# An HGRN block and a retention block on one core: one more pair of projection units in Winograd form in the first mixer, and the order of three ScalarE instructions in the MLPs

## What is computed

```python
def first_block(x, ...):
    h = rmsnorm(x, norm_mix)
    q, f, i, g = split(h @ w_in, 4)                  # w_in is 1024 x 4096
    log_f = logaddexp(log(lb), log1p(-lb) + log_sigmoid(f))
    k = (1 - lb) * sigmoid(-f)
    o = hgrn2_chunk_scan(silu(q) * 128 ** -0.5, k, i, log_f)   # 8 heads of 128
    x = x + (headnorm(o) * out_norm * silu(g)) @ w_out
    a = relu(rmsnorm(x, norm_mlp) @ w1)
    x = x + (a * a) @ w2
    return rmsnorm(x, norm_final)

def second_block(x, ...):                            # convolution and retention
    h = x + hybrid_mixer(rmsnorm(x, norm1), ...)
    h = h + sq_relu_mlp(rmsnorm(h, norm2), w_up, w_down)
    return rmsnorm(h, final_norm)
```

## Time and profile before

| | |
|---|---|
| median of 3 runs | 2258.19 us (2257.88 to 2261.65) |
| profiled execution: time, span | 2260.37 us, 2258.6 us |
| mean granted TensorE clock | 0.998 |
| busy: TensorE | 2244.6 us, 99%, 10744 instructions |
| busy: VectorE | 1682.2 us, 74% |
| busy: GpSimd | 1256.8 us, 56% |
| busy: ScalarE | 951.9 us, 42% |
| chain that ended last | TensorE 95%, VectorE 3%, VectorE's queue 1% |

### The profile page before, as it was taken

How to read it: one execution, slowest core, us unless ns; L and a number is a source line. 1 busy time by engine, 2 the same in 40 slices (tenths; PEclk the granted TensorE clock), 3 DMA queues, 4 the chain that set the end, 5 groups by cost and what they waited for, 6 DMA issues and landing times.

```text
span 2258.6 us, 32472 instructions
## 1 busy us (share of the span) xinstructions
PE 2244.6 (99%) x10744; PEld 1879.4 (83%) x10744; DVE 1682.2 (74%) x2355; ACT 951.9 (42%) x1565; POOL 1256.8 (56%) x1420
## 2 busy tenths in 40 slices
PE   9999999999999999999999999999999999999998
PEld 7888888888888888888888888888888888888887
DVE  7887887856878777876666877765787787787766
ACT  6355544424634533543432224322453454344433
POOL 4544552344556566655546666763556665666562
PEclk9999999999999999999999999999999999999999
DMA  4011111023264556455313111112335645554553
GB/s 158 29 38 38 33 34 47 29 93 130 94 229 144 180 173 214 149 177 187 114 55 121 66 43 41 48 56 103 121 136 181 214 148 177 186 198 142 196 198 140
DMA packets 60020, 274.46 MB, mean 122 GB/s; under 512 B 7184, under 2 KB 10384, under 8 KB 42000
## 3 DMA queue, kind: packets, MB, share of 16 engines
q1 hardware_dynamic: 58800, 270.51, 34.5%
q10 hardware_dynamic: 1120, 2.65, 0.3%
HBM read 211.27 MB, written 61.87 MB: 121 GB/s over the span
## 4 chain that ended last, share of the span: by engine, by line
PE 95%; DVE 3%; DVEq 1%; ACT 0%; issue 0%; DMA 0%; SPq 0%; ACTq 0%; POOL 0%; POOLq 0%
PE prod_ps L1466 8%; PE prod_ps L1467 8%; PE prod_ps L1468 8%; PE side_ps L1467 7%; PE side_ps L1468 7%; PE side_ps L1466 7%; PE prod_ps L1052 7%; PE prod_ps L1054 7%; PE prod_ps L1053 7%; PE prod_ps L1343 3%; PE prod_ps L1345 3%; PE prod_ps L1344 3%; PE prod_ps L1333 3%; PE prod_ps L1331 3%; PE prod_ps L1332 3%; PE side_ps L1192 2%
## 5 line engine op out<-in xcount | busy, mean ns | idle before, releaser
L1052 PE MATMUL prod_ps<-operand_hi,w_hi 128*128 128x512 f32 x696 | 275.3, 396 | 2.1 <-DVE operand_lo L1971 2.1
L1054 PE MATMUL prod_ps<-operand_hi,w_lo 128*128 128x512 f32 x696 | 271.8, 391 | 0.0
L1053 PE MATMUL prod_ps<-operand_lo,w_hi 128*128 128x512 f32 x696 | 271.4, 390 | 0.0
L842 POOL TENSOR_TENSOR w_lo<-w_raw,w_hi 128x256 fp32r<-128x256 f32 x168 | 154.8, 941 | 127.4 <-ACT w_hi L3410 127.1
L842 POOL TENSOR_TENSOR w_lo<-w_s,w_hi 128x256 fp32r<-128x256 f32 x168 | 129.0, 771 | 143.0 <-ACT w_more_hi L3418 115.1
L797 POOL CAST w_hi<-w_raw 128x1024 fp32r<-128x1024 f32 x41 | 43.6, 1064 | 266.6 <-PE prod_ps L1054 177.2
L2491 DVE TENSOR_TENSOR x_res<-prod_ps,x_res 128x512 f32<-128x512 f32 x130 | 89.0, 685 | 97.6 <-PE prod_ps L1468 97.6
L801 POOL TENSOR_TENSOR w_lo<-w_raw,w_hi 128x256 fp32r<-128x256 f32 x164 | 155.5, 979 | 3.3
L1052 PEld LDWEIGHTS prod_ps<-operand_hi,w_hi 128*128 128x128 f32 x696 | 131.1, 188 | 29.1 <-DVE operand_lo L1971 2.4
L1054 PEld LDWEIGHTS prod_ps<-operand_hi,w_lo 128*128 128x128 f32 x696 | 130.9, 188 | 27.9
L1053 PEld LDWEIGHTS prod_ps<-operand_lo,w_hi 128*128 128x128 f32 x696 | 131.2, 189 | 26.2
(11 more groups left out here) (461 smaller groups left out, 6842.8 us busy)
## 6 DMA issues: line engine op xcount, KB each, us to landing
w_raw<-stream SPq DMA_DIRECT2D x202, 512.0 KB, 3.6
x_park<-x_res SPq DMA_DIRECT2D x45, 1024.0 KB, 8.1
x_res<-x_park SPq DMA_DIRECT2D x45, 1024.0 KB, 6.8
swapped<-op_park SPq DMA_DIRECT2D x39, 1024.0 KB, 5.0
op_park<-swapped SPq DMA_DIRECT2D x6, 1024.0 KB, 8.2
x_in<-x_t SPq DMA_DIRECT2D x16, 256.0 KB, 5.2
x_res<-x_t SPq DMA_DIRECT2D x8, 512.0 KB, 4.3
end_park<-x_res SPq DMA_DIRECT2D x4, 1024.0 KB, 3.8
```

What stands on the lines that cost most here:

```text
L842: return nc.gpsimd.tensor_tensor(dst, src, high.bitcast(F32), ALU.subtract)
L1052: nc.tensor.matmul(into, w_h, a_h, start=(k == 0), stop=False)
L1053: nc.tensor.matmul(into, w_h, a_l, start=False, stop=False)
L1054: last = nc.tensor.matmul(into, w_l, a_h, start=False, stop=(k == KT - 1))
```

## The change

It does two things. First, U_PAIRED1 is 4 instead of 6: units 4 and 5 of the first mixer, until now the second and third plain unit of head 1, become the first of ten pairs. The function `second_head` on TensorE runs unit 3 plainly and then pair 0 with the levels of head 0 put between its pieces. GpSimd no longer splits the units 4 and 5 plainly. VectorE makes all four operand sums, T1 to T4, ahead of level 1 and their low parts ahead of level 2, where they had been spread over the levels 3 to 6 and behind. ScalarE's `second_iteration` holds the casts, copies and gathers for pair 0, and the casts for pair 1. `scores_first` also holds for head 1: at level 6 VectorE takes the scores before it grows. The banks that the last pairs use are chosen anew. Second, in the MLPs' `far_phase` ScalarE does the relu copy ahead of the two raw casts instead of behind them; `plain_phase` keeps its order.

```diff
@@ -91,7 +91,7 @@
 UNITS = U_MLP2 + MLP_UNITS[1]
 U_PAIRED = U_IN2 + 6
 IN2_PAIRS = (U_OUT2 - U_PAIRED) // 2
-U_PAIRED1 = U_IN1 + 6
+U_PAIRED1 = U_IN1 + 4
 IN1_PAIRS = (U_G1 - U_PAIRED1) // 2
@@ -110,7 +110,7 @@
 
 
 PAIR_BANKS, PAIR_FREED = pair_banks(U_PAIRED, IN2_PAIRS, [(1, 3, 2, 0), (3, 2, 0, 1)])
-PAIR_BANKS1, PAIR_FREED1 = pair_banks(U_PAIRED1, IN1_PAIRS, [(0, 1, 3, 2), (1, 3, 2, 0), (3, 2, 0, 1)])
+PAIR_BANKS1, PAIR_FREED1 = pair_banks(U_PAIRED1, IN1_PAIRS, [(1, 0, 2, 3), (3, 2, 0, 1)])
 
 
 @dataclass
@@ -998,7 +998,6 @@
             pool.sem_inc(high_made, 2)
             split_third()
             split_unit(3, 1)
-            split_units(4, U_PAIRED1)
             for j in range(IN1_PAIRS):
                 split_paired(in1, j)
             split_unit(U_G1, 0, (in1.prod, 7 * IN1_PAIRS - 3))
@@ -1257,7 +1256,11 @@
                     newer_level(6)
                     back()
 
-                if n >= HEADS1 or n < 2:
+                if n == 1:
+                    mids = [None, None, lambda: newer_level(2), lambda: newer_level(3), None, None]
+                    ends = [lambda: newer_level(0), lambda: newer_level(1), None, lambda: newer_level(4),
+                            lambda: newer_level(5), lambda: newer_level(6)]
+                elif n >= HEADS1 or n < 1:
                     mids = [turn_v_and_last_level, turn_k, kv_then_second_level, lambda: newer_level(3), None,
                             lambda: newer_level(6)]
                     ends = [lambda: newer_level(0), lambda: newer_level(1), None, out_then_fourth_level,
@@ -1286,15 +1289,24 @@
                     if ends[j] is not None:
                         ends[j]()
 
+            def in1_pair(j, mids, ends):
+                m0, m1, m2, m3 = mids
+                e0, e1, e2, e3 = ends
+                paired(in1, j, {"P2": m0, "c11": e0, "P6": m1, "c12": e1, "P7": m2, "c22": e2, "P4": m3, "c21": e3})
+
+            def second_head():
+                mids, ends = hgrn_steps(1, 1)
+                for half in range(NH):
+                    product(3, 1, half, 0, mid=mids[half])
+                    ends[half]()
+                in1_pair(0, mids[2:6], ends[2:6])
+
             def two_heads(n):
 
                 steps = [hgrn_steps(n + k, k) for k in range(2)]
                 mids, ends = steps[0][0] + steps[1][0], steps[0][1] + steps[1][1]
                 for p in range(3):
-                    m0, m1, m2, m3 = mids[4 * p:4 * p + 4]
-                    e0, e1, e2, e3 = ends[4 * p:4 * p + 4]
-                    paired(in1, (3 * n - U_PAIRED1) // 2 + p,
-                           {"P2": m0, "c11": e0, "P6": m1, "c12": e1, "P7": m2, "c22": e2, "P4": m3, "c21": e3})
+                    in1_pair((3 * n - U_PAIRED1) // 2 + p, mids[4 * p:4 * p + 4], ends[4 * p:4 * p + 4])
 
             def in_weight(s, which, kk):
                 if which <= S2:
@@ -1438,7 +1450,7 @@
             tiles(0, 0, 0, range(KT - 2, KT), into=early_product).then_inc(prod, 1)
             norm_spread(T_NORM0 + 1, 1)
             hgrn_iteration(0, 0, mid_start=True)
-            hgrn_iteration(1, 1)
+            second_head()
             for n in range(2, HEADS1, 2):
                 two_heads(n)
@@ -2084,7 +2096,7 @@
 
                     step = hgrn_step(n, f"L{number}")
                     scores = done_step(step).rearrange("p (c t) -> p c t", c=NB)
-                    scores_first = number == LEVELS - 2 and 2 <= n < HEADS1
+                    scores_first = number == LEVELS - 2 and 1 <= n < HEADS1
                     if not scores_first:
                         grow(b, number)
                     if number == 0:
@@ -2177,6 +2189,34 @@
                 def first_pair_of(unit):
                     first_two(in1, (unit - U_PAIRED1) // 2)
 
+                if n == 1:
+                    newer_level(0)
+                    in1_combine(T1, 0, 1, T1)
+                    group(0)
+                    in1_combine(T3, 2, 1, T3)
+                    dve.drain()
+                    in1_combine(T2, 2, 1, T1)
+                    dve.drain()
+                    in1_combine(T4, 2, 0, T2)
+                    newer_level(1)
+                    in1_low(T1, 1)
+                    group(1)
+                    in1_low(T2, 3)
+                    in1_low(T3, 3)
+                    in1_low(T4, 4)
+                    newer_level(2)
+                    group(2)
+                    newer_level(3)
+                    first_pair_of(u + 1)
+                    group(3)
+                    newer_level(4)
+                    newer_level(5)
+                    group(4)
+                    group(5)
+                    newer_level(6)
+                    second(4)
+                    second(5)
+                    return
                 if 2 <= n < HEADS1:
                     level(par, LEVELS - 1)
                     if par:
@@ -2263,30 +2303,15 @@
                     third(5)
                     return
                 group(2)
-                if n == 1:
-                    in1_combine(T1, 0, 1, T1)
                 newer_level(3)
-                if n == 1:
-                    in1_combine(T3, 2, 1, T3)
                 newer_level(4)
                 group(3)
-                if n == 1:
-                    in1_combine(T2, 2, 1, T1)
                 newer_level(5)
                 group(4)
-                if n == 1:
-                    dve.drain()
-                    in1_combine(T4, 2, 0, T2)
-                if n == 1:
-                    in1_low(T1, 1)
                 newer_level(6)
                 group(5)
                 second(4)
                 second(5)
-                if n == 1:
-                    in1_low(T2, 3)
-                    in1_low(T3, 3)
-                    in1_low(T4, 4)
 
             def in1_combine(op, m, half, other):
...
@@ -3338,8 +3367,8 @@
             first_operands()
             second_iteration()
             for n in range(2, HEADS1, 2):
-                even_iteration(n, 3 * (n // 2 - 1))
-                odd_iteration(n + 1, 3 * (n // 2 - 1) + 2)
+                even_iteration(n, 3 * (n // 2) - 2)
+                odd_iteration(n + 1, 3 * (n // 2))
 
             def gate_sigmoid(j):
                 sigmoid_g(U_G1, j // 2, j % 2)
@@ -3555,9 +3584,11 @@
                     for slot in range(2):
                         high_s12(slot, summed(g, q, 1 + slot))
 
-                def both_last_highs(g, q, u):
+                def both_s34_highs(g, q):
                     for slot in range(2):
                         high_s34(slot, summed(g, q, 3 + slot))
+
+                def both_a22_highs(g, u):
                     for slot in range(2):
                         unit_free(g, u + slot)
                         high_a22(slot)
@@ -3607,7 +3638,8 @@
                     high_of(T1, g + 1, 1)
                     both_first_highs(g, 3, 11, 12)
                     squares_early(g, 3, far_h)
-                    squares_late(g, 3, 10, far_h, far_banks, between=lambda: both_last_highs(g, 11, 12))
+                    squares_late(g, 3, 10, far_h, far_banks, between=lambda: both_s34_highs(g, 11),
+                                 behind=lambda: both_a22_highs(g, 12))
 
                 def scale_new():
                     row = (G_MLP1, G_MLP2)[index]
@@ -3687,7 +3719,11 @@
                     else:
                         both_first_highs(g, r, *next_weights)
                         squares_early(g, r, h, then)
-                        squares_late(g, r, u, h, b, then, None, next_copy, lambda: both_last_highs(g, *next_weights))
+                        def last_highs():
+                            both_s34_highs(g, next_weights[0])
+                            both_a22_highs(g, next_weights[1])
+
+                        squares_late(g, r, u, h, b, then, None, next_copy, last_highs)
 
                 if index:
                     plain_phase(2, g, 3, 10, far_banks, None)
```

38 lines of the change are left out of this document (21 added, 17 removed).

## The result

| | before | after |
|---|---|---|
| median | 2258.19 us (2257.6 to 2261.65) | 2284.16 us (2283.21 to 2285.45) |
| ratio, 95% interval | | 1.0109 (1.0097 to 1.0120) |
| span of the profiled execution | 2258.6 us | 2282.6 us |
| TensorE | 2244.6 us, x10744 | 2255.2 us, x10738 |

A forecast was written before the change was run, and what follows sets the result against it. TensorE, busy for 2244.6 of 2258.6 us, was taken as the bound. Gains of 6.1 us against added waits and slow clock summed to +3.8 us on the 2258.2 median: 2262.0 us, range 2256.0 to 2266.0.

The forecast's parts named there:

- the one on the MLPs: MLPs: relu copy ahead of the casts removes TensorE's two 0.5 us waits, -0.96 us; the casts' delay costs nothing.
- a wait released by w_a_lo: Sign that the prediction is wrong: a new TensorE wait in an MLP, released by GpSimd's weight low part.
- six matmuls less: First mixer: two plain units take 96 matmuls, as a pair 90; -1.36 us.
- turn_k's wait: Third head: TensorE's wait for VectorE's level 7 goes, as low parts now run in the second head; -2.15 us.
- the slow clock behind it: Third head: eight matmul intervals at the lower clock behind turn_k's wait go with it; -1.6 us.
- wait ahead of P1, slow clock behind: First pair's start: TensorE waits from 58.98 to 65.15 us for GpSimd's first low part, +6.2; lower clock, +1.6 us.
- level 5: First pair: level 5's gather stands behind the next pair's weight casts; 0 to 1.0, taken at +0.5 us.
- level 6: First pair: level 6's gather stands behind the sigmoid of q; wait 0.9 to 1.9, taken at +1.6 us.
- the rival of 0.23: The wait ahead of level 6 also drops the clock, +1.6, front's slow stretch +3.2: 2263.6 to 2265.2 us; chance 0.23.
- four TensorE waits over 0.4 us: Kernel before: 2.1 us for VectorE, two of 0.5 us for ScalarE's MLP copy, one in the first microseconds.

The follow-up runs named there:

- e3: Kernel before with the MLPs' relu copy ahead of the two raw casts, but signalled only behind them, without the tenth pair; ratio 1.0001.
- e4: Kernel before with only one of the MLPs' two raw casts put behind the relu copy, the other still ahead, without the tenth pair; ratio 1.0002.
- x1_after_slot0_first: The whole changed kernel, with GpSimd doing slot 0's w_a_lo ahead of slot 1's w_s_lo in the far phases; 2265.99 us, ratio 1.0036.
- e2: The changed kernel with its MLP part undone, so the tenth pair alone; ratio 1.0047.
- m2: e2 with ScalarE's gathers of levels 5 and 6 moved ahead of the casts and sigmoid they stood behind; 2267.45 us, ratio 1.0034.
- m3: m2 with the front of the first pair reordered on ScalarE and VectorE, weight casts right behind the first gather; 2265.34 us, ratio 1.0026.
- m4: m3 with ScalarE's casts of S3, S4 and A22 and its fourth gather moved earlier; 2265.42 us, ratio 1.0025.
- m6: Kernel before with the MLPs' relu copy first and GpSimd doing slot 0's w_a_lo ahead of slot 1's w_s_lo; 2257.17 us, ratio 0.9990.
- m7: The first mixer of m3 with the MLPs of m6; 2262.77 us, ratio 1.0017.

## Why the prediction was wrong

**The step that failed** is the one on the MLPs: "The casts then end at about 613.8 us, and GpSimd takes up what they feed only at 618.26, so their delay costs nothing. The other eleven far phases show no TensorE wait, so nothing is to be gained there." The first sentence is true of the casts: e3 and e4 delay them at no cost. It asks only who waits for what comes later. What comes earlier was credited (0.96 us) and not asked about: what it would collide with. The 16 us lie there, and at worst the MLPs were priced at zero. The rows were at hand: the earlier trace rows has two of GpSimd's subtractions at 3.41 us in a far phase and two at 1.89 in the mixer, and the earlier trace rows the place in time. And "no TensorE wait" was read as slack. It was none: VectorE waited 15.5 us in all for that load before the change, and TensorE stood at the edge of waiting for VectorE.

The prediction named a wait released by w_a_lo as what would prove it wrong. It came two links further on, named x_res. And 0.35 us of a wait stand for 1 to 1.2 us lost, since a wait is only part of it: behind the far phase at 699 us after, TensorE falls back by 0.28 us at one matmul without a wait in the view, by 0.50 at the one with a wait of 0.34, and by the rest in smaller steps.

**The mixer, step by step.** The forecast for it was +4.8 us; with TensorE 0.33 us early at 50 us and 8.15 late at 600, +8.5 were measured.

| step | forecast | measured |
|---|---|---|
| six matmuls less | -1.36 | x10738 for x10744 |
| turn_k's wait | -2.15 | gone |
| the slow clock behind it | -1.6 | gone, but it was no sure gain (below) |
| wait ahead of P1, slow clock behind | +7.8 | 8.3 up to P2's end, with 0.57 of a wait at P5 that was forecast as none |
| level 5 | +0.5 | 0.67 and the start, 0.8 |
| level 6 | +1.6 | 1.94 and the start, 2.1 |
| slow clock behind level 6 | none | 1.8: the rival of 0.23 |

The measured steps add up to 7.9 of the 8.5 us; the rest was not taken apart.

The mechanisms were right, the first low part came at 64.64 us for 65.15. The largest term missing, 1.8 us, was a rival and named as such; it is no sure cost either, for in x1_after_slot0_first, with the same mixer and a wait of 1.90 us at the same place, the granted clock from 92 to 102 us is 1.00. The rival's case, 2263.6 to 2265.2, would have held the mixer's part; the MLPs' 16 us lie outside every case that the prediction has. It also counts four TensorE waits over 0.4 us where the view has five: the fifth, 1.5 us for VectorE at the very start, is the same in both kernels and changes no sum. In the MLPs the stage copy's wait did go at the first MLP (0.7 us, from 8.15 to 7.43 us late).

**Open**: the 1.7 us that e2, and with nearly the same mixer m2, lose in the second MLP, and m3 and m4 (0.5 us) hardly do. It is there in the new MLP order too: x1 gains 0.1 us in the second MLP where m6 and m7 gain 1.3 to 1.4. So it goes with the mixer of the change and not with that of m3, but no run tells the cause apart.

## What to carry to other kernels

When an instruction is moved ahead, ask of every engine what its new time collides with, GpSimd and VectorE with two SBUF inputs first: here a start of VectorE's sums at 0.42 us instead of 0.72 cost GpSimd 0.98 us each time. An engine without waits isn't an engine with slack: follow the engine that feeds it, and whoever feeds that, and look for idle time that ends at a load. And where a buffer's release is on such a link, do the work that releases it first; here that cost nothing, one loop for two, and gave the only kernel faster than both.
